# A low-rank gate product on four column groups, and a head norm whose squares VectorE adds before one product with ones

## What is computed

```python
def rms_norm(x, w):
    xf = x.astype(jnp.float32)
    y = xf * lax.rsqrt(jnp.mean(xf * xf, axis=-1, keepdims=True) + EPS)
    return (y * w.astype(jnp.float32)).astype(x.dtype)

def gla_branch(h, w_in, w_gate_up, gate_bias, out_norm_w):
    ...
    q, k, v, r, z, xq = split_cols(h @ w_in, [qk, qk, SEQ_WIDTH, GLA_RANK, MIX_WIDTH, XA_WIDTH])
    g = jax.nn.log_sigmoid((r @ w_gate_up + gate_bias).astype(jnp.float32)) / GLA_TAU
    o = gla_chunked(...)              # S_t = diag(exp(g_t)) S_{t-1} + k_t^T v_t ;  o_t = q_t S_t
    o = rms_norm(o, out_norm_w).reshape(b_, l_, SEQ_WIDTH)
    return o.astype(h.dtype), z, xq
```

## Time and profile before

| | |
|---|---|
| median of 3 runs | 3071.57 us (3069.75 to 3076.17) |
| span of the profiled execution | 3059.5 us |
| TensorE busy | 2831.8 us, 93% |
| GpSimd, one low part (typical) | 2.4 us |
| granted TensorE clock, mean of the span | 0.977 |

### The profile page before, as it was taken

How to read it: one execution, slowest core, us unless ns; L and a number is a source line. 1 busy time by engine, 2 the same in 40 slices (tenths; PEclk the granted TensorE clock), 3 DMA queues, 4 the chain that set the end, 5 groups by cost and what they waited for, 6 DMA issues and landing times.

```text
span 3059.5 us, 45014 instructions
## 1 busy us (share of the span) xinstructions
PE 2831.8 (93%) x17982; PEld 2326.8 (76%) x17982; DVE 1407.1 (46%) x2208; ACT 999.7 (33%) x1526; POOL 1097.9 (36%) x773
## 2 busy tenths in 40 slices
PE   6898989899999999999989888899998999899997
PEld 4566567677788678787768877899997877678885
DVE  5788364520206611402138676570634456382452
ACT  3222354222212235523225333412124455332211
POOL 0233122444233179443433423244442321244442
PEclk9999999999999999999999998999999998999999
DMA  3888111144573279332221100222222210122222
GB/s 137 266 278 265 64 42 43 61 161 140 166 217 106 94 182 258 114 97 90 90 86 65 43 3 23 69 90 90 90 91 76 81 44 22 56 89 96 92 95 76
DMA packets 130751, 324.88 MB, mean 106 GB/s; under 512 B 54144, under 2 KB 54784, under 8 KB 129808
## 3 DMA queue, kind: packets, MB, share of 16 engines
q1 hardware_dynamic: 96128, 221.90, 22.3%
q0 software_dynamic: 30096, 88.21, 10.1%
q10 hardware_dynamic: 4352, 12.26, 1.0%
HBM read 288.32 MB, written 33.95 MB: 105 GB/s over the span
## 4 chain that ended last, share of the span: by engine, by line
PE 69%; DVE 17%; ACT 4%; DMA 4%; issue 3%; POOL 3%; DVEq 1%; ACTq 0%; SPq 0%; POOLq 0%
PE ps L270 17%; PE ps L273 17%; PE ps L275 17%; DMA d_pb<-arena 2%; POOL ring_r L363 2%; DVE h L603 1%; PE ps L1781 1%; PE ps L925 1%; PE ps L1520 1%; PE ps L583 1%; ACT high L372 1%; PE ps L1612 1%; PE ps L2196 1%; PE ps L2908 1%; DVE x L600 1%
## 5 line engine op out<-in xcount | busy, mean ns | idle before, releaser
L363 POOL TENSOR_TENSOR ring_r<-ring,high 128x1024 fp32r<-128x1024 f32 x335 | 833.6, 2489 | 1387.0 <-ACT high L372 1386.9
L270 PE MATMUL ps<-h_hi,high 128*128 128x512 f32 (+1 forms) x2104 | 734.3, 357 | 51.4 <-POOL ring_r L363 27.5
L275 PE MATMUL ps<-h_hi,ring_r 128*128 128x512 f32 (+1 forms) x2104 | 660.1, 348 | 0.0
L372 ACT ACTIVATE high<-ring 128x1024 fp32r<-128x1024 f32 x367 | 387.9, 1057 | 827.5 <-PE ps L270 698.5
L273 PE MATMUL ps<-h_r,high 128*128 128x512 f32 (+1 forms) x1912 | 641.2, 345 | 0.0
L270 PEld LDWEIGHTS ps<-h_hi,high 128*128 128x128 f32 x2104 | 399.0, 190 | 128.7 <-issue 51.0
L275 PEld LDWEIGHTS ps<-h_hi,ring_r 128*128 128x128 f32 x2104 | 368.8, 190 | 53.3
L273 PEld LDWEIGHTS ps<-h_r,high 128*128 128x128 f32 x1912 | 363.3, 190 | 41.1 <-issue 1.4
L273 PE MATMUL ps<-f_r,high 128*128 128x264 f32 (+1 forms) x960 | 294.9, 321 | 0.0
L270 PE MATMUL ps<-f_hi,high 128*128 128x264 f32 (+1 forms) x896 | 270.7, 316 | 2.2 <-POOL ring_r L363 1.8
L275 PE MATMUL ps<-f_hi,ring_r 128*128 128x264 f32 (+1 forms) x896 | 230.9, 316 | 0.0
(11 more groups left out here) (484 smaller groups left out, 4235.1 us busy)
## 6 DMA issues: line engine op xcount, KB each, us to landing
ring<-in_units SPq DMA_DIRECT2D x402, 512.0 KB, 3.3
d_ca<-arena POOLq DMA_DIRECT2D x16, 640.0 KB, 8.6
arena<-d_ca POOLq DMA_DIRECT2D x16, 640.0 KB, 6.2
arena<-d_q POOLq DMA_DIRECT2D x32, 256.0 KB, 7.7
d_pb<-arena POOLq DMA_DIRECT2D x16, 512.0 KB, 10.5
arena<-d_pb POOLq DMA_DIRECT2D x16, 512.0 KB, 4.0
arena<-d_ca POOLq DMA_DIRECT2D x16, 512.0 KB, 5.0
arena<-d_k POOLq DMA_DIRECT2D x128, 64.0 KB, 4.2
```

The source lines that it names most:

```text
L270: part = mm(acc, hi[:, cols], self.x_hi(k)[:, t0:t0 + tn], start=(k == 0), stop=False)
L275: ins = mm(acc, w[:, cols], self.x_hi(k)[:, t0:t0 + tn], start=False, stop=(k == self.kt - 1))
L363: eng.tensor_tensor(b.ring_r[:, slot, :], b.ring[:, slot, :], self.high[:, (j + self.flip) % 2, :], ALU.subtract).then_inc(b.unit_lo, 1)
L372: b.nc.scalar.activation(self.high[:, (j + self.flip) % 2, :], b.ring[:, u % RING, :], ACT.Copy).then_inc(b.unit_hi, 1)
```

## The change

`GlaRank` widens each of the 8 weight tiles from 16 to 32 columns with zeros, and puts the product of tile 4i + j into partitions 32j to 32j + 31 of the bank, so that four neighbouring products write four different column groups. The four partial sums are not added there: `w_up` is repeated four times along the rows (with zeros between), and the products that follow (L1049) sum over all 128 rows. `w_rank` gets a buffer of its own, and the loads are larger: `w_rank` 128 KB for 64, `w_up` 256 KB for 32.

The new `HeadNorm` squares all four tiles into three buffers, VectorE adds them (three additions), and one product with ones follows. That product moves behind the first half of the z tile that stands in its step. The root moves behind ScalarE's casts of that step (and behind the gate's exponentials of the next head but one, where there are any).

```diff
 class GlaRank(Stage):
...
-        for k in range(KD):
+        for i in range(KD // QUARTERS):
             for part, h in enumerate((b.h_hi, b.h_r)):
-                ins = b.nc.tensor.matmul(b.ps[0:RANK, 0, :], m.w_rank[:, k, :], h[:, k, 0:L1].bitcast(F32),
-                                         start=(k + part == 0), stop=(k + part == KD))
+                for j in range(QUARTERS):
+                    k = i * QUARTERS + j
+                    ins = b.nc.tensor.matmul(b.ps[BAND * j:BAND * (j + 1), 0, :], m.w_rank[:, k, :],
+                                             h[:, k, 0:L1].bitcast(F32), start=(i + part == 0),
+                                             stop=(i + part == KD // QUARTERS))
...
+class HeadNorm(Rms):
+    def squares(self, act):
...
+        for k in range(self.n):
+            if k == 3:
+                act.wait_ge(b.added, at["added"] + 1)
+            b.nc.scalar.activation(self.spot(k), self.x(k), ACT.Square).then_inc(b.squared, 1)
+
+    def add(self, dve, k):
+        b, at = self.b, self.at
+        dve.wait_ge(b.squared, at["squared"] + k + 1)
+        if k > 1:
+            dve.wait_ge(b.added, at["added"] + k - 1)
+        b.nc.vector.tensor_tensor(self.spot(0), self.spot(0), self.spot(k), ALU.add).then_inc(b.added, 1)
+
+    def tensor(self, pe):
...
+        pe.wait_ge(b.added, at["added"] + self.n - 1)
+        b.nc.tensor.matmul(b.ps[:, self.banks[0], :], b.ones[:, :], self.spot(0), start=True, stop=True
+                           ).then_inc(b.summed, 1)
+
+    def roots(self, act):
+        b, at = self.b, self.at
+        act.wait_ge(b.summed, at["summed"] + 1)
...
 class Gla(Stage):
...
-            mm(b.ps[:, 2 + h % 2, :], m.w_up[0:RANK, h * P:(h + 1) * P], m.rank[0:RANK, :],
+            mm(b.ps[:, 2 + h % 2, :], m.w_up[:, h * P:(h + 1) * P], m.rank[:, :],
...
-            if n >= 5 and n % 4 == 1:
-                self.rms[(n - 5) // 4].tensor(pe)
-            for s, half in halves[:-1]:
+            for i, (s, half) in enumerate(halves[:-1]):
                 z.half_tensor(pe, s, half)
+                if n >= 5 and n % 4 == 1 and i == 0:
+                    self.rms[(n - 5) // 4].tensor(pe)
...
             for s in self.PLAN[n]:
                 z.high_unit(act, s + 1)
+            if n >= 5 and n % 4 == 1:
+                self.rms[(n - 5) // 4].roots(act)
...
             if n >= 4 and n % 4 == 0:
-                self.rms[(n - 4) // 4].scalar(act)
+                self.rms[(n - 4) // 4].squares(act)
...
+            if n >= 5 and n % 4 == 1:
+                norm = self.rms[(n - 5) // 4]
+                norm.add(dve, 1)
+                norm.add(dve, 2)
             if 1 <= n <= self.steps:
...
+            if n >= 5 and n % 4 == 1:
+                norm.add(dve, 3)
...
+        m0.squares = [b.sq[:, 0, 0:L1], b.sq[:, 1, 0:L1], view(24064, L1)]
```

More of the change, by code:

```diff
@@ L972, in vector @@
                     b.nc.vector.tensor_tensor(z, z, b.ps[:, 6 + c, :], ALU.mult).then_inc(self.gated, 1)
+BAND = 32
+QUARTERS = P // BAND
 class GlaRank(Stage):
@@ L996, in scalar, with __init__, spot @@
         act.wait_ge(self.ranked, 1)
-        b.nc.scalar.activation(m.rank[0:RANK, :], b.ps[0:RANK, 0, :], ACT.Copy).then_inc(self.rank_kept, 1)
+        b.nc.scalar.activation(m.rank[:, :], b.ps[:, 0, :], ACT.Copy).then_inc(self.rank_kept, 1)
+class HeadNorm(Rms):
+    def __init__(self, b, spots, o, saved, stay):
+        super().__init__(b, lambda k: o[:, k, :], DV // P, FULL, DV, EPS, lambda k: b.col("gla_out_norm_w", k),
+                         lambda k: o[:, k, :], [0], [saved], stay)
+        self.spots = spots
+        b.norms["summed"] += 1 - self.n
+        b.norms["added"] += self.n - 1
+    def spot(self, k):
+        return self.spots[k if k < 3 else 1]
+    def squares(self, act):
+        b, at = self.b, self.at
+        for s, v in self.needs:
+            act.wait_ge(s, v)
+        if at["summed"]:
+            act.wait_ge(b.summed, at["summed"])
+        for k in range(self.n):
[9 more added lines that the diff above has]
+    def tensor(self, pe):
+        b, at = self.b, self.at
+        for s, v in self.stay:
+            pe.wait_ge(s, v)
+        pe.wait_ge(b.added, at["added"] + self.n - 1)
+        b.nc.tensor.matmul(b.ps[:, self.banks[0], :], b.ones[:, :], self.spot(0), start=True, stop=True
+                           ).then_inc(b.summed, 1)
+    def roots(self, act):
+        b, at = self.b, self.at
+        act.wait_ge(b.summed, at["summed"] + 1)
+        if at["inverted"]:
+            act.wait_ge(b.inverted, at["inverted"])
+        b.nc.scalar.activation(b.root[:, 0:L1], b.ps[:, self.banks[0], :], ACT.Sqrt, bias=b.eps[self.eps],
+                               scale=1.0 / self.width).then_inc(b.rooted, 1)
 class Gla(Stage):
@@ L1031, in __init__ @@
             last = min(4 * h + 5, self.steps)
-            self.rms.append(Rms(b, lambda k, o=o: o[:, k, :], DV // P, FULL, DV, EPS,
-                                lambda k: b.col("gla_out_norm_w", k), lambda k, o=o: o[:, k, :], [0],
-                                [(self.saved, 4 * h + 4)], [(self.masked, last), (self.token_keys, last)]))
+            self.rms.append(HeadNorm(b, m.squares, o, (self.saved, 4 * h + 4),
+                                     [(self.masked, last), (self.token_keys, last)]))
         self.done = (self.multiplied, z.body_outs * z.iters)
@@ L3368, in build @@
         m0.ktok = view(32640, 2, P)
-        m0.w_rank = view(32896, KD, RANK)
+        m0.w_rank = b.sb("w_rank", [P, KD, BAND])
         m0.w_up = view(33024, 512)
         m0.decay = view(33536, GLA_HEADS, 8)
+        m0.squares = [b.sq[:, 0, 0:L1], b.sq[:, 1, 0:L1], view(24064, L1)]
         m0.silu = [b.p[:, :, :].rearrange("p a t -> p (a t)"), b.sq[:, 2, 0:L1]]
@@ L3388, in build @@
         small.append((m0.w_rank[:, :, :], a["w_rank"]))
-        small.append((m0.w_up[0:RANK, :], a["w_up"]))
+        small.append((m0.w_up[:, :], a["w_up"]))
         loads_in = b.loads_in = (loaded, 16 * len(small))
@@ L3977 @@
     }
+    band = ((0, 0), (0, BAND - RANK))
+    arrays["w_rank"] = np.pad(arrays["w_rank"], ((0, 0),) + band)
+    arrays["w_up"] = np.tile(np.pad(arrays["w_up"], band[::-1]), (QUARTERS, 1))
     arrays.update(s5_arrays(i))
```

## The result

The changed kernel takes 3079.48 us (median of 11 runs, 3074.29 to 3086.27) and the kernel before 3070.49 (11 runs, 3064.99 to 3076.17): a ratio of 1.0031, with a 95% interval of 1.0021 to 1.0042. It is slower by 9 us. The forecast was 3063.5, and the range ended at 3072.5. The profiled execution took 3077.42 us, 2.9 more than its span of 3074.5.

A forecast was written before the change was run, and what follows sets the result against it. TensorE, busy for 93% of the span, was taken as the bound. The terms +0.7 - 0.6 - 4.7 - 3.5 summed to -8.1 us, so 3071.6 became 3063.5 us, with a range of 3057.5 to 3072.5.

The forecast's parts named there:

- The start, +0.7: TensorE's first product: the larger loads delay the load it waits for by 0.7 us, bounds 0 and 1.4.
- The rank product, -0.6: Rank product: 4 us for 13.85; d_vm's landing lets 2.6 us through, less 2.0 for half clock behind the wait.
- Heads 0 to 2, -4.7: Norms of heads 0, 1 and 2: one product of ones each gains 1.6, 1.5 and 1.6 us.
- a bound that I had named: Head norms: a head gains 0 if GpSimd holds up an addition as long as the cast that took 2.62 us.
- the clock's fall at a norm: Rival at heads 0 and 1: half clock behind waits grown from 1.25 to 2.3 us, 2.0 us each; 3067.5, chance 0.09.
- Head 3 and the stage's end, -3.5: Head 3 to out0's tile 0: it ends at 625.1 us, before at 628.6, despite head 3's later root.
- three of them, 6.6: SplitZ ahead of the last times_z: three GpSimd low parts get in between, each holding VectorE for 2.2 us.
- starved at unit 22 or 23: Rival in SplitZ: GpSimd's low part waits for VectorE's run; +0.6 (+0.9) in place of -3.5; 3067.7, chance 0.20.
- the wait of 9: Stage's end: TensorE waits 9 us for out0's second unit, in place of its earlier wait of 10 us.

The follow-up runs named there:

- e9: Kernel before with the new rank product, VectorE's waits for GpSimd and early times_z in SplitZ, w_rank and w_up loads on their own semaphore: 3059.2 us.
- e16: Kernel before with only SplitZ altered: VectorE waits for GpSimd's low parts, and times_z stands earlier: 3060.5 us, ratio 0.9966.
- e3: Kernel before with only the change's larger loads of w_rank and w_up; products and norms as before: 3073.2 us, ratio 1.0013.
- e7: Changed kernel plus one VectorE copy of 512 columns ahead of SplitZ: 3079.2 us, ratio 1.0033 to the kernel before.
- e8: Changed kernel with head 3's norm as in the kernel before: 3068.6 us, ratio 0.9996 to the kernel before.
- e13: Changed kernel plus one VectorE copy of 32 columns ahead of SplitZ: 3083.8 us (one run).
- e4: Changed kernel, with VectorE waiting at four places in SplitZ for GpSimd's low parts: 3068.4 us, ratio 0.9992 to the kernel before.
- e1: Kernel before with only the new rank product and its larger loads; head norms as before: 3069.0 us, ratio 1.0000.
- e2: Kernel before with only the new head norms; rank product and loads as before: 3080.8 us, ratio 1.0031.
- e12: Changed kernel plus a VectorE reciprocal of 32 columns ahead of every second cast of SplitZ: 3069.1 us, ratio 0.9994 to the kernel before.
- e15: Changed kernel plus two VectorE copies, of 512 and 32 columns, ahead of SplitZ: 3081.5 us (one run).
- e10: Kernel before with new rank product, SplitZ waits for GpSimd, early times_z, and heads 0 to 2's new norm with parts placed later: 3052.9 us.

## Why the prediction was wrong

By the terms of the sum, before to changed, as measured on the pieces of the table:

- **The start, +0.7: right.** The first product came 0.56 us later. Behind it the first norm of x ran partly at half clock, so that its reciprocal began 1.8 us later still, 38.77 for 36.40. I took that for the loads' doing, and e9's expectation rests on it; but it shows in eight of thirteen profiles with these loads ahead of the first product and in e16, which has the loads of before. e3's median says 3 us for the loads, with an interval of 1 to 7; e9 doesn't bear it out.
- **The rank product, -0.6: right in its mechanism, too small.** 3.5 us for 13.85; `d_vm` landed 11.5 us after the rank product's start (11.2 before), TensorE was idle for 8.04 us and came back at half clock (granted 0.50 from 324 to 328 us), the first eight instructions in 3.68 us. From rank to up it gained 2.7. What I left out: half clock is not only added; the stretch that the kernel before had at 355.9 us, 3.4 us long (0.66 on the mean of 355 to 360), was gone (1.00). That part was luck: of the fourteen profiles with this rank product only those of the changed kernel, e7 and e8 lack it, and the gain of the middle profile is 1.2 us. The Trainium skill (TensorEngine Tiling (Array Packing), Theoretical Speedup) speaks of up to four times for 32 columns: the trace has 13.85 against 3.5, and so agrees.
- **Heads 0 to 2, -4.7: wrong, +1.1.** At the norm itself two heads did what I worked out: -1.2 and -1.4 for -1.6 and -1.5, measured at the L1144 behind it. At head 2 GpSimd held the third addition for 2.39 us, a bound that I had named: +0.3. What fails is that the waits of 2.41 and 2.83 us bring half clock behind them at heads 0 and 2, +1.5 and +1.6 over the next step. I had given the clock's fall at a norm a chance of 0.09, at heads 0 and 1. Which head it strikes isn't settled by the wait: in e13, with the same code for the norms, it came behind the wait of 2.41 us at head 1 (granted 0.50 from 492 to 496 us) and not behind the 2.83 us at head 2 (1.00 from 537 to 541).
- **Head 3 and the stage's end, -3.5: wrong, +6.4.** The step that failed is "three of them, 6.6": that GpSimd's low parts get in between. VectorE and TensorE came to SplitZ as I had laid it out: the reciprocal came 7.3 us behind the product of ones where I had 7.7. But unit 22's request was lost (13.93 us), and out0's second unit as well (7.00). The rival *starved at unit 22 or 23* had the first of these, at a price of +0.6, and took the second to come through; the second is 4.6 us longer than a low part of 2.4. Where all come through, in e4, the stage's end is 2.8 us shorter than before and TensorE's wait is 8.90 us: the -3.5 and the wait of 9 were right for the case that didn't happen.

The four terms as measured add up to +5.4 us, where the medians differ by 9.0 (6.4 to 12.9 by the interval). The pair of profiles doesn't place the other 3.6; the luck from rank to up is some 1.4 of it.

What e1, e2, e4, e8 and e12 show together is that the second starved low part is the loss: without starving (e4, e12) the change is level with the kernel before, which has one, and still does not gain what its parts were to give. The Trainium skill (SBUF — State Buffer, SBUF: two separate sides) has whoever starts first hold the port pair for an instruction. Were the other one next in turn, that would cost GpSimd one instruction; that was my reading. The skill doesn't say who is next, and 13.93 us and e15's 14.36 over some 25 instructions show that GpSimd need not be, as the earlier trace rows did.

What stays open is why one request is lost and the next one served. Neither its moment nor its place in the run decides it alone in these traces.

## What to carry to other kernels

Where VectorE has a long unbroken run and TensorE waits for something that GpSimd makes meanwhile, give GpSimd its turn: a wait of VectorE for that result, or a short instruction of another kind, was worth 10 to 11 us in the changed kernel. Only low parts that somebody waits for need it: six kernels here starve one for 6.6 us and lose nothing. Work taken off TensorE gains only if what replaces it is ready in time; place the product where its sums are done. In e10 that took 7.2 us off the 16 steps; ahead of that, waits of 2.41 and 2.83 us brought half clock that cost 3.1 us, more than the 2.6 that two heads had won. One profile of each kernel is not enough for the difference of two: compare it piece by piece, and learn the spread of each piece from runs of the same code.

## What was not expected of the hardware

- Four column groups of 32 in full float32, 128x32x512: 32 instructions in 3.5 us, about four times faster than on one group of 16 (13.85). A group of eight starts every 0.86 us and lasts 1.04 to 1.07; a single instruction lasts 0.59 in both kernels.
- A request of GpSimd can wait for VectorE's whole run, 14.36 us, and for 7.00 us again at the run's next stretch; with a reciprocal of 0.34 us ahead of every second cast no low part took over 2.84 us.
- A wait of TensorE of 2.41 us was followed by half clock at head 0 (442 to 446 us), and the same wait at head 1 was not (1.00 from 487 to 492 us). In e13 it was at head 1 too (0.50 from 492 to 496).
